# ConvFFN down projection: seven half products per pair of row tiles in place of whole products, four norm blocks in place of three

## The reference, cut to what matters

```python
def conv_ffn(xn, prev, wup, cw, cb, wdown):
    hid = xn @ wup                                    # 1024 -> 5632
    hp = jnp.concatenate([prev, hid], axis=1)
    c = cb
    for j in range(3):                                # causal depthwise conv
        c = c + hp[:, j:j + t] * cw[j]
    gate, val = jnp.split(c, 2, axis=-1)
    return (gelu(gate) * val) @ wdown, hp[:, t:]      # 2816 -> 1024

# per layer, sandwich norms:
x = x + rmsnorm(mixer(rmsnorm(x, g[0])), g[1])
x = x + rmsnorm(conv_ffn(rmsnorm(x, g[2])), g[3])     # layer 0 then norms x for layer 1
```

## Time and profile before

| | |
|---|---|
| median of 3 runs | 4157.53 us |
| the profiled execution | 4153.73 us, span 4151.9 us |
| TensorE busy | 3773.5 us (91%), mean granted clock 0.963 |
| VectorE busy | 1996.3 us (48%) |
| ScalarE, GpSimd busy | 815.7 us (20%), 516.6 us (12%) |
| down projection (line 338) | 646.6 us of TensorE in two layers, 2112 matmul records |
| up projection (line 299) | 408.1 + 291.1 + 145.5 + 145.5 + 47.2 us |

### The profile page before, as it was taken

How to read it: one execution, slowest core, us unless ns; L and a number is a source line. 1 busy time by engine, 2 the same in 40 slices (tenths; PEclk the granted TensorE clock), 3 DMA queues, 4 the chain that set the end, 5 groups by cost and what they waited for, 6 DMA issues and landing times. The chain is left out here.

```text
span 4151.9 us, 79805 instructions
## 1 busy us (share of the span) xinstructions
PE 3773.5 (91%) x35200; PEld 2817.8 (68%) x35200; DVE 1996.3 (48%) x3258; ACT 815.7 (20%) x1859; POOL 516.6 (12%) x432
## 2 busy tenths in 40 slices
PE   7998687888699999999988999999648999999998
PEld 4887566666466888865666777777535688886566
DVE  8441676666435666640124464746613566664001
ACT  6110344333121110010011222222212100001000
POOL 1221000000011222200011010101001122220001
PEclk9999899999899999999998999999768999999999
DMA  2222011010111111123321111111183111112223
GB/s 78 84 84 94 30 36 38 28 35 27 66 74 40 46 43 42 43 96 109 115 99 69 55 38 45 51 40 46 55 334 113 56 43 42 43 43 98 110 98 127
DMA packets 97216, 291.80 MB, mean 70 GB/s; under 512 B 37224, under 2 KB 52968, under 8 KB 88040
## 3 DMA queue, kind: packets, MB, share of 16 engines
q1 hardware_dynamic: 96872, 286.70, 19.5%
HBM read 237.71 MB, written 48.95 MB: 69 GB/s over the span
## 5 line engine op out<-in xcount | busy, mean ns | idle before, releaser
L338 PE MATMUL ps<-sb_big,sb_w 128*128 128x384 f32 (+1 forms) x2112 | 646.6, 468 | 1.2 <-ACT sb_tmp L428 1.2
L338 PEld LDWEIGHTS ps<-sb_big,sb_w 128*128 128x128 f32 x2112 | 400.2, 190 | 241.6 <-ACT sb_tmp L428 2.2
L299 PE MATMUL ps<-sb_h,sb_w 128*128 128x272 f32 x1672 | 408.1, 392 | 1.4 <-ACT sb_tmp L428 1.4
L299 PEld LDWEIGHTS ps<-sb_h,sb_w 128*128 128x128 f32 x1672 | 317.5, 190 | 67.7 <-issue 2.3
L299 PE MATMUL ps<-sb_x,sb_w 128*128 128x272 f32 x1216 | 291.1, 392 | 0.0
L471 DVE TENSOR_TENSOR sb_tmp<-sb_tmp 128x384 f32<-128x384 f32 (+1 forms) x63 | 34.8, 552 | 526.7 <-ACT sb_tmp L370 525.0
L299 PEld LDWEIGHTS ps<-sb_x,sb_w 128*128 128x128 f32 x1216 | 231.0, 190 | 47.6
L573 DVE SCALAR_TENSOR_TENSOR sb_big<-sb_tmp,sb_big 128x1024 f32<-128x1024 f32 (+1 forms) x176 | 204.0, 1159 | 13.4 <-issue 0.3
L2080 PE MATMUL ps<-sb_h,sb_w 128*128 128x384 f32 (+1 forms) x576 | 186.9, 468 | 0.0
L1099 PE MATMUL ps<-sb_x,sb_w 128*128 128x272 f32 x768 | 183.8, 392 | 0.0
L269 PE MATMUL ps<-sb_h,sb_w 128*128 128x384 f32 (+1 forms) x576 | 178.6, 470 | 3.9 <-DVE sb_tmp L548 2.1
(11 more groups left out here) (345 smaller groups left out, 6128.0 us busy)
## 6 DMA issues: line engine op xcount, KB each, us to landing
sb_w<-wdown SPq DMA_DIRECT2D x46, 1408.0 KB, 6.0
sb_w<-wup SPq DMA_DIRECT2D x88, 512.0 KB, 4.3
sb_w<-wqkv SPq DMA_DIRECT2D x36, 512.0 KB, 3.8
sb_big<-kT SPq DMA_DIRECT2D x8, 2304.0 KB, 14.6
sb_big<-vc SPq DMA_DIRECT2D x8, 2304.0 KB, 16.3
sb_w<-wrkv SPq DMA_DIRECT2D x24, 512.0 KB, 5.4
rkv_scratch<-sb_big SPq DMA_DIRECT2D x18, 544.0 KB, 6.3
sb_big<-rkv_scratch SPq DMA_DIRECT2D x16, 544.0 KB, 3.6
```

What stands on the lines that cost most here:

```text
L299: mm = pe.matmul(m.ps[:, 2 * HOME[f][p] + e, 0:PIECE], w, rhs[:, k, e * PIECE:(e + 1) * PIECE], start=(k == 0 and p not in ("P2", "P3")), ...
L338: mm = pe.matmul(m.ps[:, u % 6, 0:n], wdt[u % 2][:, f, :], hid[:, f, t0:t0 + n], start=(f == 0), stop=(f == FT - 1))
```

## The change

The output tiles of the down projection go in pairs, and tokens in two halves `u` of 544, each in two columns of 272 (`PIECE`). The inner dimension of 22 tiles is cut in two halves of 11 (`HF`). For each pair of output tiles and each half of the tokens this is a 2 x 2 by 2 x 2 block product, and it is made of seven products of 11 matmuls with 272 tokens (`seventh`) in place of eight: 8 steps `n` of 7 products. Step n handles output tiles 2(n mod 4) and 2(n mod 4) + 1, and token half n // 4.

- The weights of a step come in four loads of 704 KB (W11, W21, W12, W22), each behind the semaphore of what used its buffer last.
- GpSimd makes four weight sums of 128x1408 in each step (`W3`, `W2`, `W21`, `W2` again).
- VectorE makes four token sums for each half of the tokens (`hidden_sum`): those of half 0 when hidden tiles 20 and 21 are done, those of half 1 inside step 3.
- ScalarE copies the banks of P1 and P2 out; VectorE combines the other five with these copies (`combine`).
- The norm blocks are four of 272 tokens. The first two are normed in steps 4 and 5, the last two after the last product; statistics are taken in pieces of 68 lanes. In layer 0 the second norm of the last two blocks takes its sum over channels by matmuls on each squared tile (`late_statistic`), which accumulate in one bank with a single first flag.
- The residual is loaded back in halves to parts of `m.H` and of `hid` that are free, not to `m.X`.
- In `rwkv_core` the gate projections and `normal_key(0)` stand ahead of the small tables, and `pv` is counted on the semaphore of the gate weights.

The core of the diff:

```diff
-            for b, (t0, n) in enumerate(TB):
                 for k in range(KT):
-                    u = KT * b + k
...
-                    for f in range(FT):
...
-                        mm = pe.matmul(m.ps[:, u % 6, 0:n], wdt[u % 2][:, f, :], hid[:, f, t0:t0 + n], start=(f == 0), stop=(f == FT - 1))
+            def seventh(n, p):
+                u = n // 4
+                lhs, rhs = {"P1": (W11, lambda k: half(u, 0, 0)[:, k, :]), "P7": (W3, lambda k: tsum(3, k, k + 1)[:, 0, :]),
+                            "P2": (W12, lambda k: half(u, 1, 0)[:, k, :]), "P6": (W2, lambda k: tsum(2, k, k + 1)[:, 0, :]),
+                            "P5": (W21, lambda k: half(u, 0, 1)[:, k, :]), "P4": (W22, lambda k: tsum(4, k, k + 1)[:, 0, :]),
+                            "P3": (W2, lambda k: half(u, 1, 1)[:, k, :])}[p]
...
+                for k in range(HF):
+                    if (n, p, k) == (0, "P7", HF - 1):
+                        pe.wait_ge(hidden, FT + 1)
+                    mm = pe.matmul(m.ps[:, BANK[n, p], 0:PIECE], lhs[:, k, :], rhs(k), start=(k == 0 and p not in ("P2", "P3")),
+                                   stop=(k == HF - 1), skip_group_check=True)
...
+            for n in range(NDOWN):
+                for p in DOWN:
+                    seventh(n, p)
+                    if (n, p) == (4, "P1"):
+                        block_statistic(0, 0)
+                    if n in (4, 5) and p == "P7":
+                        block_spread(0, n - 4)
+                    if (n, p) == (4, "P7"):
+                        block_statistic(0, 1)
...
             token_sums()
...
+                if f == FT - 2:
+                    for j in (3, 1, 2, 4):
+                        hidden_sum(j, 0, 0, HF - 1)
+            for j in (3, 1, 2):
+                hidden_sum(j, 0, HF - 1, HF)
+            hidden_sum(4, 0, HF - 1, HF).then_inc(hidden, 1)
...
+                combine(n, "P6")
+                combine(n, "P7")
+                block_add(n, 0)
+                if n == 3:
+                    hidden_sum(3, 1, 0, HF).then_inc(hidden, 1)
+                    hidden_sum(1, 1, 0, HF)
...
+            for n in range(NDOWN):
+                pool.wait_ge(a11_in, 16 * (n + 1))
+                pool.wait_ge(a21_in, 16 * (n + 1))
...
+                pool.tensor_tensor(W3, W11, W21, ALU.subtract).then_inc(sums_done, 1)
...
+                pool.tensor_tensor(W2, W22, W3, ALU.subtract).then_inc(sums_done, 1)
+                pool.tensor_tensor(W21, W21, W22, ALU.add).then_inc(sums_done, 1)
...
+                pool.wait_ge(product, down(n, "P6"))
+                pool.drain()
+                pool.tensor_tensor(W2, W12, W2, ALU.subtract).then_inc(sums_done, 1)
...
-            pe.wait_ge(consts, 9 * 16)
+            for g in range(3):
+                gates(0, g)
+            pe.wait_ge(consts, 8 * 16)
             for l in range(6):
...
             mm.then_inc(small_ps, 1)
-            for g in range(3):
-                gates(0, g)
```

More of the change, by code:

```diff
@@ new lines, in tail, with tsum @@
+        XIN = [m.H[:, :, HALF + j * PIECE:HALF + (j + 1) * PIECE] for j in range(2)]
+        XIN += [hid[:, KT:2 * KT, j * PIECE:(j + 1) * PIECE] for j in range(2)]
+        OUT = [m.H[:, :, DB[j]:DB[j] + PIECE] for j in range(2)]
+        OUT += [hid[:, 0:KT, j * PIECE:(j + 1) * PIECE] for j in range(2)]
+        half = lambda u, r, c: hid[:, r * HF:(r + 1) * HF, DB[2 * u + c]:DB[2 * u + c] + PIECE]
+        def tsum(j, lo, hi):
+            at_plane = (j - 2) * HF + lo
+            return tiles(m.lanes, 0, 1, PIECE) if at_plane == 32 else tiles(m.x, at_plane * PIECE, hi - lo, PIECE)
@@ L348, in _, with block_statistic @@
-            statistic(1, 0, NBLK - 1)
-            spreading(1, 0, NBLK - 1)
-            if norms[1] == 2:
-                statistic(1, 1, NBLK - 1)
-                spreading(1, 1, NBLK - 1)
+            def block_statistic(n, b):
+                if n == 0:
+                    pe.wait_ge(summed[0], SUMS0 + 14 * (b // 2) + 13 + b % 2)
+                    acc = ACC1[:, b % 2, :]
+                else:
+                    pe.wait_ge(summed[1], SUMS0 + (KT - 1) * (b + 1))
+                    acc = ACC2[:, 0, :]
+                for j, (t0, w) in enumerate(dsubs):
+                    mm = pe.matmul(m.ps[0:w, 6, j:j + 1], acc[:, t0:t0 + w], m.ones[:, 0:1], start=True, stop=True)
+                mm.then_inc(stat, 1)
@@ new lines, in late_statistic, with block_spread @@
+            def late_statistic(b, k):
+                bank = 6 if b == 2 else SPARE2
+                pe.wait_ge(squared, NU + KT * b + k + 1)
+                for j, (t0, w) in enumerate(dsubs):
+                    mm = pe.matmul(m.ps[0:w, bank, 8 + j:9 + j], SQ3[b - 2][:, k, t0:t0 + w], m.ones[:, 0:1],
+                                   start=(k == 0 and j == 0), stop=(k == KT - 1), skip_group_check=True)
+                if k == KT - 1:
+                    mm.then_inc(stat, 1)
+            def block_spread(n, b):
+                pe.wait_ge(inverted, stat_at(n, b))
+                if b == 3:
+                    wait_taken(pe, NDOWN - 1, "P7")
+                    if n == 1:
+                        pe.wait_ge(applied, spread_at(0, 3))
+                else:
+                    pe.wait_ge(applied, spread_at(0, 2) if (n, b) == (1, 2) else spread_at(n, b) - 1)
+                for j, (t0, w) in enumerate(dsubs):
+                    mm = pe.matmul(m.ps[:, spread_bank(n, b), t0:t0 + w], DRINV[n][:, j:j + 1].broadcast_to([w, P]),
+                                   m.ident[0:w, 0:w], start=True, stop=True)
+                mm.then_inc(spread, 1)
@@ L401, in _ @@
-            collect(0)
-            root(0, 0, 2)
+                    act.wait_ge(added, KT * b + k + 1)
+                    square(1, b, k, m.X[:, k, t0:t0 + n]).then_inc(squared, 1)
+            for b in range(NBLK):
+                for k in range(KT):
+                    take(b, k)
+                    if b and k == 0:
+                        root(0, b - 1)
+                    if b and k == 2:
+                        squares(b - 1)
+                    if b and k == 5:
+                        root(1, b - 1)
@@ new lines, in block_normed @@
+            def block_normed(b):
+                dve.wait_ge(spread, spread_at(1, b))
+                if b == 2:
+                    dve.wait_ge(m.x_moved, stored + 64)
+                rows = XIN[b] if b < 2 else XS[b - 2]
+                for k in range(KT):
+                    ins = dve.scalar_tensor_tensor(out=m.H[:, k, DB[b]:DB[b] + PIECE], in0=rows[:, k, :],
+                                                   scalar=m.ng[:, g_next * KT + k:g_next * KT + k + 1],
+                                                   in1=m.ps[:, spread_bank(1, b), 0:PIECE], op0=ALU.mult, op1=ALU.mult)
+                ins.then_inc(applied, 1)
@@ new lines, in combine @@
+            def combine(n, p):
+                u2, u3, c22 = out_of(n, 0, 1), out_of(n, 1, 0), out_of(n, 1, 1)
+                out, left, op = {"P6": (u2, u2, ALU.add), "P7": (u3, u2, ALU.add), "P5": (c22, u3, ALU.add),
+                                 "P4": (u3, u3, ALU.subtract), "P3": (u2, u2, ALU.add)}[p]
+                dve.wait_ge(product, down(n, p))
+                if p == "P6":
+                    wait_taken(dve, n, "P1")
+                dve.drain()
+                dve.tensor_tensor(out, left, m.ps[:, BANK[n, p], 0:PIECE], op).then_inc(parted, 1)
```

568 lines of the change are left out of this document (398 added, 170 removed).

## The result

The changed kernel takes 4110.63 us (median of 4 runs, 4101.89 to 4115.87) against 4156.05 us of the kernel before in the same set: a ratio of 0.9888, 95% interval [0.9869, 0.9908]. A second set, experiment `e0_after_again`, gave 4109.90 us and 0.9883 [0.9867, 0.9899]. The forecast was 4088 us, range 4073 to 4106, faster. The direction holds; the size doesn't: 45 us were gained and not 69, and the time lies above the range.

A forecast was written before the change was run, and what follows sets the result against it. Matmul time on TensorE was taken to bound both down projections. Layer 0 (-31.7 us), layer 1 (-32.3), tails (-1.0) and RWKV start (-4.0) sum to -69.0 us, so 4088 us was forecast, range 4073 to 4106.

The forecast's parts named there:

- layer 0's tail: After layer 0's last product: additions, squares with their matmuls and scalings take 21.5 us, 0.5 us less than before.
- place 1: Start of each down projection: GpSimd's weight sums delay VectorE's small token sums, so TensorE waits 1.5 us a layer.
- place 2: Step 3 to step 4: token sums and weight sums delay block 0's reciprocal and spread; 4 us a layer.
- TensorE's products: Down projections: 56 products of 11 matmuls at 5.05 us each, 282.6 us a layer.
- Weight sums in the steps: GpSimd's four sums a step, 3.55 us each, meet their deadlines; steps 0 to 2 and 5 to 7 run without waits.
- Statistics and spreads: Norm work on TensorE between products, 0.7 us each: 7.0 us in layer 0, 4.2 us in layer 1.
- The RWKV start: Gate weights and gates go first, so VectorE's scan starts 4.0 us earlier.
- Layer 1's tail: After layer 1's last product: final store of 272 tokens instead of 320, 0.5 us less.
- Exclude each other more: Rival, chance 0.18: VectorE and GpSimd block each other more, 6 us at the start and 13 at step 3; 4100 to 4116.
- Nothing collides: Rival, chance 0.17: VectorE and GpSimd don't hold each other up, both tight places cost nothing; 4076.5 us.
- GpSimd bounds every step: Rival, chance 0.04: weight sums last so long that TensorE waits in each step; slower, 4203 us at 12.5 us a sum.
- products don't get shorter: Rival, chance 0.02: bank changes cost 0.7 us at each end of a product, 78 us gone, time unchanged.

The follow-up runs named there:

- e0_after_again: The changed kernel unaltered, profiled and timed once more (the repeat): 4109.90 us, ratio 0.9883 to the kernel before.
- e7_all: Changed kernel with step 0's weight sums behind small token sums, last large token sum in step 4, late sums by wide matmuls: 4075.03 us, ratio 0.9820.
- e5_few_stats: Changed kernel without six of the eight late sums of each of blocks 2 and 3 (norms wrong): 4104.99 us, layer 0's tail 23.3 us.
- e2_rwkv_only: Kernel before with only the new start of the RWKV core: 4153.45 against 4158.02 us, ratio 0.9988.
- e3_place1: Changed kernel with GpSimd's second and third weight sum of step 0 waiting for the last small token sum: 4087.78 us, one run.

## Why the forecast was wrong in size

The time came out above the range because three terms were too small: the lower clock behind a wait, which had no term at all, the late sums in layer 0's tail, and the wait of place 1. In the repeat they make about 11, 5.8 and 5.3 us of the 25 us by which the two sums differ. The wait of place 2 gives 2.6 us back, and the last 5 us lie in small waits, in the statistics and in stages that the change leaves alone.

- **TensorE's products: right.** 5.05 us were forecast, 5.04 measured.
- **Weight sums in the steps: right.** 3.17 to 3.36 us against 3.55; steps 1, 2, 6 and 7 show no wait of TensorE, and GpSimd bounds nothing.
- **Statistics and spreads: near.** Without the places the stretches take 291.35 and 287.71 us (`e7_all`) against 289.6 and 286.8. The mean for one of a pair was about right (0.46 and 0.85 us against 0.7 each); 1.2 us in layer 0 are small waits.
- **Place 1: mis-sized, 1.5 us against 6.4 and 6.3 us.** The mechanism stood in the prediction. What failed was the choice of 1.5 us between 0, 2.6 and 6: the sums start when tile 21 is gated, in the same moment as the small sums, and the third stands directly behind the second, so nothing spoke for the middle. The order of the queues already said "two". The runs with no, one and two sums gave 297.1, 298.8 and 303.5 us. That the price for two sums (6 us) comes near 6.4 is luck: it was a price for the wait alone, two sums of 3.55 us and 1.0 us that no row gives, less 2.0 us of air. The wait is 4.15 us, and the rest is the clock.
- **Place 2: right in its chain, short by 1.5 and 2.6 us.** The wait of 2.93 us is less than the 4 forecast (4.5 in layer 0 with the second norm). The rest is the lower clock behind it, 3.2 us.
- **The lowered clock after a wait had no term.** In the first profile it is 1.7 us at place 1 and 3.2 to 3.4 us at place 2, in the repeat 2.3 to 2.5 and 3.2 us. In the repeat that makes 11 of the 25 us by which the two sums differ (69.0 forecast, 44.2 measured), more than any other term. The prediction counted a wait at its length and nothing more; it named a clock below 1.00 as a sign of being wrong, but gave it no rival and no price.
- **Layer 0's tail: wrong, -0.5 us against +5.3 us.** The step "squares and their matmuls until 13 us" put the late sums at no more than their squares. 128 records at 0.115 us are 14.7 us of TensorE, which ends 6.8 us behind the last square, and they are on the path to the end (`e5_few_stats`). The added work was 16 groups of four small matmuls; it should have been priced as such, 7.4 us even at the 0.46 us of the full clock, and more at the 0.62 that the tail of before already showed. A tail over 3 us longer was the other sign that the prediction had named.
- **The RWKV start: right, within its scatter.** -4.0 forecast; the scan came 4.9 and 4.1 us earlier in the two profiles of after and 3.5 us in the mean of all profiles, and `e2_rwkv_only` gave -4.6 us in the medians.
- **Layer 1's tail: right** within 0.3 us.
- **The rivals.** *Exclude each other more* (4100 to 4116) is what happened in time (4110.63 us) but only in one of its two reasons: place 1 cost its 6 us, place 2 cost 6 and not 13, and the clock and the tail, which it didn't have, made up the time. *Nothing collides* fell, *GpSimd bounds every step* and *products don't get shorter* too.

The Trainium skill (SBUF — State Buffer, "Who interferes with whom") was read rightly and used too mildly: the trace agrees that the instruction which issued first holds the other for its whole length (3.40 us for 0.43 us of work, `e3_place1` against after).

## What to carry to other kernels

Where two engines that exclude each other are released by the same event, count the whole queue of the one that wins, and order the short operations on which TensorE waits ahead of the long ones by a semaphore; one changed constant gave over 6 us a layer. A wait of TensorE can cost more than its length: the waits of 2.9 and 4.15 us cost 1.5 to 2.2 times theirs here, so look at the granted clock of the product behind a wait. Small matmuls that are added to a tail can be the path there: price them by their number, at the clock that the tail already shows.
